# Seven half products instead of eight in the gate/up pairs of two feed-forward stages

## The reference

```python
h = h + 0.5 * swiglu(rmsnorm(h, g1), w_gate, w_up, w_down)   # stage 0 (layer 0), stage 2 (layer 1)
h = h + mixer(rmsnorm(h, gm));  h = h + cross_attn(rmsnorm(h, gx), mem_n, ...)
h = h + 0.5 * swiglu(rmsnorm(h, g2), ...)                    # stage 1 (layer 0), stage 3 (layer 1)
swiglu(x, w_gate, w_up, w_down) = (silu(x @ w_gate) * (x @ w_up)) @ w_down     # 1024 -> 2816 -> 1024
```

## Time and profile before

| | |
|---|---|
| median of three runs | 2180.11 us |
| profiled execution, span from first to last instruction | 2178.7 us |
| granted clock of TensorE, mean | 0.999 |
| PE busy, matmuls | 2169.0 us, 10582 |
| DVE / ACT / POOL busy | 1042.9 / 455.5 / 1529.9 us |
| weight stream moved | 202.03 MB of 214.12 |

### The profile page before, as it was taken

The page is one execution under the profiler, slowest core; times in us unless marked ns, Lnnn a source line. Parts: engine busy times, 40 slices in busy tenths (PEclk is TensorE's granted clock), DMA queues, the critical chain, the costliest instruction groups (busy, mean ns, idle before and its releaser), DMA issues. The chain is left out here.

```text
span 2178.7 us, 30347 instructions
## 1 busy us (share of the span) xinstructions
PE 2169.0 (100%) x10582; PEld 1793.5 (82%) x10582; DVE 1042.9 (48%) x1386; ACT 455.5 (21%) x816; POOL 1529.9 (70%) x1530
## 2 busy tenths in 40 slices
PE   9999999999999999999999999999999999999998
PEld 7888888888988888888888888886878888888887
DVE  6556795695444352233352224356872543222333
ACT  4001212034223210001131111134362332111112
POOL 7777787667964776776776677685756657667764
PEclk9999999999999999999999999999999999999999
DMA  5233323223431333333333333232322222333332
GB/s 196 95 96 116 115 97 122 91 77 98 129 92 59 102 97 96 96 96 97 111 102 96 96 96 97 96 102 78 102 88 92 78 68 96 97 97 97 97 97 82
DMA packets 115350, 214.12 MB, mean 98 GB/s; under 512 B 12832, under 2 KB 14400, under 8 KB 115008
## 3 DMA queue, kind: packets, MB, share of 16 engines
q1 hardware_dynamic: 111024, 202.03, 29.3%
q10 hardware_dynamic: 4240, 10.99, 1.5%
HBM read 208.77 MB, written 4.19 MB: 98 GB/s over the span
## 5 line engine op out<-in xcount | busy, mean ns | idle before, releaser
L443 PE MATMUL ps<-x,w_split 128*128 128x512 f32 (+1 forms) x2854 | 1105.4, 387 | 1.1 <-DVE x L1754 0.7
L445 PE MATMUL ps<-x,w_split 128*128 128x512 f32 (+1 forms) x2854 | 1097.2, 384 | 0.0
L444 PE MATMUL ps<-x,w_split 128*128 128x512 f32 (+1 forms) x2854 | 1096.9, 384 | 0.0
L401 POOL TENSOR_TENSOR w_split<-w_raw,w_split 128x512 fp32r<-128x512 f32 x758 | 1026.8, 1355 | 64.2 <-ACT w_split L1463 1.1
L391 POOL TENSOR_SCALAR w_split<-w_raw 128x512 fp32r<-128x512 f32 x754 | 495.1, 657 | 560.5 <-PE ps L445 556.4
L443 PEld LDWEIGHTS ps<-x,w_split 128*128 128x128 f32 x2854 | 536.0, 188 | 118.2 <-issue 10.3
L444 PEld LDWEIGHTS ps<-x,w_split 128*128 128x128 f32 x2854 | 536.2, 188 | 107.0 <-issue 1.4
L445 PEld LDWEIGHTS ps<-x,w_split 128*128 128x128 f32 x2854 | 536.1, 188 | 107.0
L1881 DVE TENSOR_TENSOR x<-arena,x 128x512 fp32r<-128x512 f32 x88 | 119.2, 1365 | 218.6 <-ACT x L1322 218.6
L1831 DVE TENSOR_TENSOR tu<-ps,rstd 128x512 f32<-128x512 f32 x88 | 60.7, 689 | 315.3 <-PE ps L445 315.3
L1260 ACT ACTIVATE sg<-tg 128x512 f32<-128x512 f32 x88 | 55.6, 632 | 668.5 <-DVE tg L1828 667.2
(11 more groups left out here) (303 smaller groups left out, 1332.5 us busy)
## 6 DMA issues: line engine op xcount, KB each, us to landing
w_raw<-in_stream SPq DMA_DIRECT2D x758, 256.0 KB, 2.6
arena<-in_memT ACTq DMA_DIRECT2D x2, 1024.0 KB, 6.4
s_tables<-kv ACTq DMA_DIRECT2D x4, 512.0 KB, 3.2
arena<-s_tables ACTq DMA_DIRECT2D x4, 512.0 KB, 4.3
out<-h ACTq DMA_DIRECT2D x6, 256.0 KB, 2.2
h<-in_xT SPq DMA_DIRECT2D x4, 256.0 KB, 5.3
h<-in_xT SPq DMA_DIRECT2D x2, 512.0 KB, 6.9
w_raw<-in_stream SPq DMA_DIRECT2D x5, 128.0 KB, 5.8
```

Source lines behind the costliest of these rows:

```text
L401: pool.tensor_tensor(lo, x, hi.bitcast(F32), ALU.subtract).then_inc(split_ready if half else S("half_split"), 1)
L443: pe.matmul(dst, wh, xh, start=start, stop=False)
L444: pe.matmul(dst, wh, xl, start=False, stop=False)
L445: return pe.matmul(dst, wl, xh, start=False, stop=stop)
```

## The change

Let A11, A21 be the first four channel chunks of the first and second 256 tokens, A12, A22 the last four chunks; B11 and B21 the first and last four chunks of the gate's weights, B12 and B22 those of the up's. From pair 3 on (`SEVEN = {1: 3, 3: 3}`: stages 1 and 3, pairs 3 to 21) a pair is formed by seven products of 4 chunks x 3 matmuls of 256 columns, in this order: A11 B11 (M1), S1 T1 (M5), S2 T2 (M6, added onto M1 in the same bank), S4 B22, S3 T3, A12 B21 (M2, a bank of its own), A22 T4, with the token sums S1 = A21 + A22, S2 = S1 - A11, S4 = A12 - S2, S3 = A11 - A21 and the weight sums T1 = B12 - B11, T2 = B22 - T1, T3 = B22 - B12, T4 = B21 - T2.

- **Weights.** `W` gets 6 more half units. ACT makes all seven high parts (before: POOL). DVE forms T1, T2 and T4 in PSUM banks 6, 7, 0 and their low parts; POOL forms T3 in a new SBUF tile and the low parts of B11, B22, T3 and B21. SP loads the halves in the order B11, B12, B22, B21, each when its raw half has been used.
- **Results.** ACT keeps three partial results in `sq` (c1, c5, c2), DVE adds them (`join`: C12, C22, C11), then `up_out`, `gate_out` and, after ACT's SiLU, the product.
- **Token sums.** During the norm ACT writes the gained `h` once more in float32 (8 copies); DVE forms the four sums and their low parts (1024 columns each), ACT their high parts. They lie in the chunks that the first hidden chunks used, so hidden chunks 0 to 3 are split only in the last pair.
- **Order.** The first down block takes its 8 outputs in another order (`DOWN_FIRST_SEVEN`). The tables of stage 1 go behind down chunks 10 and 16. Several semaphores of short steps are merged into `act_step` and `dve_step`, and DMA scratch is made smaller, with no other effect on the order.

The core of the diff, in the order PE, SP, POOL, ACT, DVE as in the file:

```diff
+            def seven(f, p):
+                g, u, n = FFN_AT[f] + 2 * p, FFN_AT[f] + 2 * p + 1, 3 * (seven_of(f, p) - 1)
+                again = p > SEVEN[f]
+                sp.wait_ge(S("half_split"), g - 1)
+                if again:
+                    sp.wait_ge(S("w_sum"), n + 1)
+                load(g, g % 2, 0)
+                sp.wait_ge(S("half_split"), u - 1)
+                load(u, u % 2, 0)
+                if again:
+                    sp.wait_ge(split_ready, g - 1)
+                    sp.wait_ge(S("w_sum"), n + 2)
+                else:
+                    sp.wait_ge(split_ready, u - 1)
+                load(u, u % 2, 1)
+                sp.wait_ge(split_ready, u - 1 if again else g - 1)
+                if again:
+                    sp.wait_ge(S("w_sum"), n + 3)
+                load(g, g % 2, 1)
...
+            def seven_prepare(f, p):
+                n = 7 * seven_of(f, p)
+                def low(name, high, sem):
+                    src = t3[:] if name == "T3" else raw_of(f, name)
+                    pool.wait_ge(S("u_hi"), n + high)
+                    pool.tensor_tensor(unit(f, name, 1), src, unit(f, name, 0).bitcast(F32), ALU.subtract
+                                       ).then_inc(sem, 1)
+                low("B11", 1, S("half_split"))
+                for name in ("B12", "B22"):
+                    pool.wait_ge(*raw_sem(f, p, name))
+                pool.tensor_tensor(t3[:], raw_of(f, "B22"), raw_of(f, "B12"), ALU.subtract).then_inc(S("w_sum3"), 1)
+                low("B22", 4, split_ready)
+                low("T3", 5, S("half_split"))
+                low("B21", 6, split_ready)
...
+                product(c21, "B11", tokens(1, 1), start=True).then_inc(S("m_done"), 1)
+                pe.wait_ge(S("u_lo"), 3 * q + 1)
+                pe.wait_ge(S("up_ready"), FC * f + p - 1)
+                if first:
+                    pe.wait_ge(S("s_lo"), n + 1)
+                product(c12, "T1", summed("S1"), start=True).then_inc(S("m_done"), 1)
+                pe.wait_ge(S("u_lo"), 3 * q + 2)
+                pe.wait_ge(S("m_kept"), 3 * q + 1)
+                if first:
+                    pe.wait_ge(S("s_lo"), n + 2)
+                product(c21, "T2", summed("S2")).then_inc(S("m_done"), 1)
+                pe.wait_ge(split_ready, at + 1)
+                pe.wait_ge(S("m_kept"), 3 * q + 2)
+                if first:
+                    pe.wait_ge(S("s_lo"), n + 3)
+                product(c12, "B22", summed("S4"), stop=True).then_inc(S("half_done"), 1)
+                pe.wait_ge(S("half_split"), at + 2)
+                pe.wait_ge(S("m_kept"), 3 * q + 3)
+                if first:
+                    pe.wait_ge(S("s_lo"), n + 4)
+                product(c21, "T3", summed("S3")).then_inc(S("block_done"), 1)
+                pe.wait_ge(split_ready, at + 2)
+                if not first:
+                    pe.wait_ge(S("m_joined"), 3 * q)
+                product(second, "B21", tokens(1, 2), start=True, stop=True).then_inc(S("half_done"), 1)
+                pe.wait_ge(S("u_lo"), 3 * q + 3)
+                pe.wait_ge(S("m_joined"), 3 * q + 2)
+                product(c21, "T4", tokens(2, 2), stop=True).then_inc(S("block_done"), 1)
...
+                if n in FFN_NORM and FFN_NORM.index(n) in SEVEN:
+                    sums_high(FFN_NORM.index(n), ("S1", "S2"))
...
+                    if name in ("B11", "T1", "T2"):
+                        if p > at:
+                            act.wait_ge(S("m_done"), 3 * (q - 1) + ("B11", "T1", "T2").index(name) + 1)
+                    else:
+                        act.wait_ge(S("half_done") if name in ("B22", "B21") else S("block_done"),
+                                    b - 1 if name in ("B22", "T3") else b)
+                    act.activation(unit(f, name, 0), src, ACT.Copy).then_inc(S("u_hi"), 1)
...
+                sums_high(f, ("S4", "S3"))
+                for p in range(at - 1):
+                    silu(p // 2, p % 2)
+                for name in ("B11", "T1", "T2", "B22"):
+                    high(at, name)
+                silu((at - 1) // 2, (at - 1) % 2)
+                for name in ("T3", "B21"):
+                    high(at, name)
+                for p in range(at, FC):
+                    high(p, "T4")
+                    if p > at:
+                        silu((p - 1) // 2, (p - 1) % 2)
+                    more = p + 1 < FC
+                    keep(p, "c1")
+                    if more:
+                        high(p + 1, "B11")
+                    keep(p, "c5")
+                    if more:
+                        high(p + 1, "T1")
+                    keep(p, "c2")
+                    if more:
+                        for name in ("T2", "B22", "T3", "B21"):
+                            high(p + 1, name)
...
+                    sums(FFN_NORM.index(n))
+                    sums_low(FFN_NORM.index(n), ("S1", "S2"))
...
+                def join(p, name):
+                    q, b = seven_of(f, p), FFN_AT[f] + 2 * p
+                    c11, c21, c12, c22 = gate_up(p)
+                    if name == "C12":
+                        dve.wait_ge(S("half_done"), b + 1)
+                        dve.wait_ge(S("m_kept"), 3 * q + 3)
+                        ins = dve.tensor_tensor(c12, c12, kept(p, "c2"), ALU.add)
+                    elif name == "C22":
+                        dve.wait_ge(S("block_done"), b + 1)
+                        ins = dve.tensor_tensor(c22, c21, kept(p, "c5"), ALU.add)
+                    else:
+                        dve.wait_ge(S("block_done"), b + 2)
+                        ins = dve.tensor_tensor(c11, second, kept(p, "c1"), ALU.add)
+                    ins.then_inc(S("m_joined"), 1)
+                def up_out(p):
+                    s = p % 2
+                    dve.wait_ge(S("m_joined"), 3 * seven_of(f, p) + 2)
+                    dve.wait_ge(S("hid_done"), FC * f + p - 1)
+                    dve.tensor_tensor(tu[:, s, :], ps[:, BANKS[2 * s + 1], :], rstd[:], ALU.mult
+                                      ).then_inc(S("up_ready"), 1)
+                def gate_out(p):
+                    s = p % 2
+                    dve.wait_ge(S("m_joined"), 3 * seven_of(f, p) + 3)
+                    dve.tensor_tensor(tg[:, s, :], ps[:, BANKS[2 * s], :], rstd[:], ALU.mult
+                                      ).then_inc(S("gate_ready"), 1)
+                def product(p):
+                    s = p % 2
+                    dve.wait_ge(S("up_ready"), FC * f + p + 1)
+                    dve.wait_ge(S("silu"), FC * f + p + 1)
+                    dve.tensor_tensor(hid[:, p, :], sg[:, s, :], tu[:, s, :], ALU.mult).then_inc(S("hid_done"), 1)
+                for p in range(at - 1):
+                    gate(p // 2, p % 2)
+                add(at, "T1")
+                add(at, "T2")
+                sums_low(f, ("S4", "S3"))
+                add(at, "T4")
+                low(at, "T1")
+                low(at, "T2")
+                gate((at - 1) // 2, (at - 1) % 2)
+                for p in range(at, FC):
+                    more = p + 1 < FC
+                    if p > at:
+                        join(p - 1, "C11")
+                        gate_out(p - 1)
+                    low(p, "T4")
+                    if more:
+                        add(p + 1, "T1")
+                    if p > at:
+                        product(p - 1)
+                    if more:
+                        add(p + 1, "T2")
+                        low(p + 1, "T1")
+                        add(p + 1, "T4")
+                        low(p + 1, "T2")
+                    join(p, "C12")
+                    join(p, "C22")
+                    up_out(p)
+                    if not more:
+                        dve.wait_ge(S("hid_done"), FC * f + 4)
+                        low_part(0)
+                        low_part(1)
+                join(FC - 1, "C11")
+                gate_out(FC - 1)
+                product(FC - 1)
+                low_part(2)
+                low_part(3)
```

More of the change, by code:

```diff
@@ L160 @@
 OUT_NORM = [2, 3, 6, 7]
+SEVEN = {1: 3, 3: 3}
+TABLES_BEHIND = (10, 16)
+SEVEN_BEFORE = {f: sum(FC - at for g, at in SEVEN.items() if g < f) for f in range(5)}
+SUM_BANKS = {"T1": 6, "T2": 7, "T4": 0}
+SECOND_BANK = 1
+HALF_T = T // 2
 XQ_BASE, OD_BASE = [13, 36], 21
@@ L232, with seven_units, seven_of, seven_at @@
 A_XPT = A_XP + 4 * T
+A_SUMS, A_GAINED = 6 * T, 14 * T
+def seven_units(f):
+    own, other = FFN_AT[f] % 2, 1 - FFN_AT[f] % 2
+    return {"B11": (8, 9), "T1": (10, 11), "T2": (12, 13), "B22": (4 * own, 4 * own + 2),
+            "T3": (4 * own + 1, 4 * own + 3), "B21": (4 * other, 4 * other + 2), "T4": (4 * other + 1, 4 * other + 3)}
+SEVEN_HELD = {"S1": 4, "S2": 6, "S4": 0, "S3": 2}
+def seven_of(f, p):
+    return SEVEN_BEFORE[f] + p - SEVEN[f]
+def seven_at(f):
+    return sorted(SEVEN).index(f)
+def is_seven(b):
+    return any(FFN_AT[f] + 2 * at <= b < FFN_AT[f] + 2 * FC for f, at in SEVEN.items())
```

(55 more changed lines are left out.)

244 lines of the change are left out of this document (185 added, 59 removed).

## The result

The changed kernel takes 2166.82 us in the median of four runs (2165.80 to 2170.73); the kernel before, run beside it, 2180.12. The ratio is 0.9942, with a 95% interval of 0.9928 to 0.9956. So the change gains 13.3 us, where 25.6 were forecast. The median lies 0.2 us inside the upper end of 2149 to 2167, in the part that belonged to rival A; the mean of the four, 2167.5, lies 0.5 us outside it. The profiled execution is the longest of the four: 2170.73 us, span 2168.9.

The account below looks back on a forecast made before the run. TensorE, busy 2169.0 of 2178.7 us, was taken as the bound: number of matmuls times their step. A gain of 30.5 us less 4.8 for edges is 25.7, so 2154.5 us was forecast, range 2149 to 2167.

Parts of the forecast that it names:

- rival A: One product in each pair waits 0.2 to 0.5 us, at product 3 or 7; 2160 to 2172 us; chance 0.22.
- Part 1: TensorE's matmuls: a pair falls from 10.88 to 10.07 us, 0.80 us gained in each of 38 pairs, 30.5 us.
- Rival C: Each product's first matmul pays 0.10 us, 0.70 us a pair; about 2181 us, no change; chance 0.04.
- Part 2: What the other engines must have ready in time within one new pair; no stall per pair was taken.
- I take no stall per pair: In seven-product pairs, TensorE never waits; the smallest margins were 0.3 to 0.5 us for c1, 0.7 for C22.
- rival B: T1 and product of every pair each meet a POOL subtraction, 1.82 us each; pair 10.8 to 11.15 us; chance 0.08.
- landing range: In each pair, the load of B12 lands 2.6 us after SP issues it, between 2.3 and 3.0.
- Part 3: Losses at the edges of stages 1 and 3: 2 x (0.9 + 1.2 + 0.3) = 4.8 us.
- the term for the first pair: First seven-product pair of each stage: B12 of pair 4 loads late, products 5 and 7 wait; 1.2 us (0 to 2).
- Start edge: Norm before each stage: two long DVE operations delay POOL's split of tile 3, TensorE waits 0.9 us (0 to 3).
- End edge: End of each stage: low parts of hid 0 and 1 meet POOL's split of the first down block; 0.3 us (0 to 1.5).
- Tables: Stage 1's angle tables on DVE, moved behind down tiles 10 and 16, cost nothing; with less lead 8.4 us each.

Follow-up runs that it names:

- x1: The changed kernel with SP loading B12 once T3's sum has read it, instead of after T3's low part: 2159.61 us, ratio 0.9904.
- x2: The changed kernel with POOL's low part of B11 waiting for DVE's product of the pair before: 2162.30 us, ratio 0.9916.
- x5: The changed kernel with DVE's product, pairs 4 to 20, waiting until POOL has made the next pair's low part of B11: 2195.44 us, ratio 1.0068.
- x4: The changed kernel with pair 2's gate out (DVE) and SiLU (ACT) earlier, low parts of S4 and S3 later, around pair 3: 2158.25 us, ratio 0.9900.
- x7: x6 with DVE's low parts of S1 and S2 moved from the norm to behind the first two pairs' gates: 2155.05 us, ratio 0.9884.
- x3: The changed kernel with TensorE's pairs 4 to 21 as a hardware loop over two pairs instead of written out: 2163.88 us, ratio 0.9925.
- x8: x7 with x3's hardware loop for TensorE's pairs 4 to 21: 2155.46 us, ratio 0.9883.
- x9: x7 with the sums' low parts spread over the first two pairs and c2 kept before T1's copy in pair 3: 2158.05 us, ratio 0.9896.
- x6: The changed kernel with the edits of x1 and x4 together: 2155.22 us, ratio 0.9882.

## Why the forecast was off by half

**The matmuls (Part 1)** were right to 0.01 us: 10.08 us a pair against 10.07, at full granted clock in every pair. Rival C (0.10 us per product) is refuted by the 84 even steps.

**The order within a pair (Part 2)** was right: counted from the start of the pair at 819.86, T1 at 2.2 to 2.9 (2.1 to 2.8 forecast), product 2.8 to 3.5 (2.7 to 3.4), both at 0.70 and 0.68 us. Rival A's small wait in every pair does not exist; the time fell into its range for other reasons. (That range was added up some 2 us low: 0.3 to 0.6 a pair give 2162 to 2173.) That the median lies inside 2149 to 2167 is luck, since two terms were too small by 7.2 and 8.5 us in the profiled execution, 2168.9 us of span against 2153.0 forecast.

**"I take no stall per pair" failed.** I gave the product 0.2 us to spare before low B11; it was 0.19 at most, and in four pairs it was gone. But that is not the step that failed: I priced one lost port as "C22 ends at 8.4 to 8.5, still just in time", and in the four pairs in which the product alone loses it, C22 ends at 8.1, in time. What I left out is a load so late that T1 itself starts behind low B11 (2.89 us into the pair). Then T1 loses the port, and the product behind it as well: rival B's two prices in one pair, C22 at 9.8, 1.34 us. I had the earlier trace rows' landing range of 2.3 to 3.0 us and took it as a limit; it was taken with at most one instruction fetch in each of these stages, and the change itself brings 13 or 14. The term I left out is 7.2 us in the profiled execution (no pair of x1 shows it, and those of x2 0.18 us each). Rival B's price per pair was good: with the product late in every pair, x5 takes 11.0 us a pair, where B had 10.8 to 11.15. Its sum, at most 2195 against 2195.4, is partly chance: x5 loses 5.7 us against the kernel before in its pairs 4 to 20 and 9.3 in the two first pairs, for which B's sum had no such term.

**The edges (Part 3): the term for the first pair failed**, 1.2 us each forecast, 5.6 and 5.3 measured, 8.5 us over both stages. I followed ACT there and only one thing on it, T3's copy behind the SiLU. That showed where I said, at products 5 and 7 (2.0 and 1.8 us together, where I had 1.2). I did not write out DVE's queue ahead of pair 3, where the low parts of S4 and S3 (4.12 us for two, both against POOL) stand between T2 and gate out. That brings the wait at product 2 and, through SiLU and three copies, the 2.2 us at product 3. x4, which changes only this order, shortens the two first pairs by 7.7 us together.

**Start edge**: 0.9 forecast, 0.65 measured, and x7 shows its cause, DVE's low parts against POOL's split. **End edge**: 0.3 forecast, 0 found. **Tables**: nothing, as forecast.

So of the 12.3 us that are missing in the median, 8.5 are the first pairs, and the start and end edges give 1.1 back. That leaves 4.9 for long pairs and slow last matmuls, where the profiled execution, the longest, has 7.2 and 1.6; the others were not traced, so how this splits in them is inferred. x1's median fits: it is 7.2 less, 5.3 without its shorter pair 3.

## What to carry to other kernels

Write out every engine's queue for the first round of a new steady state as well as for the steady state itself: what is left of the old order stands in front of it, and here it cost 10.9 us in two rounds. Where two engines share a port, ask of each operation what falls behind it when it loses: here the last one in a row had the slack (1.8 us instead of 0.7 cost nothing), the one before it had not, since it makes both lose. The price of a late load was 0.18 us without the port and 1.34 with it, so fix the order by an earlier load or a wait. Code that is written out brings its own DMA traffic, which has to be counted among the transfers it runs beside. And where one execution differs from the next by 1 us or so at the kernel's ends, an account by stage says more than the difference of two medians.

## What the runs showed of the hardware that was not expected

The granted clock of TensorE fell to the level of 1.2 GHz for some 3.4 us in pair 3 of stage 3 of x1, right behind the two waits of products 2 and 3 (1.47 and 2.29 us from one matmul to the next). The 3.4 us are an estimate from the second row, 4.40 us at 0.61. The matmuls of 256 columns then started 0.21 us apart instead of 0.12, which is why pair 3 stayed at 15.24 us. Columns as above, with the clock behind POOL's:

```profile
1829.00:1835.60 6.60, 3.40 (x27) 2.99 (x25) 5.67 (x8) 2.55 (x6) 1.86 (x3) 1.00 0.15 56
1835.60:1840.00 4.40, 4.40 (x24) 4.40 (x25) 3.47 (x5) 2.14 (x5) 4.19 (x4) 0.61 0.29 81
1840.00:1845.00 5.00, 5.00 (x44) 5.00 (x43) 2.82 (x7) 2.31 (x4) 3.74 (x3) 1.00 0.46 142
```

In x2, x3 and x5 the first pairs of both stages show it too, behind two waits like these (1.0 to 1.3 and 2.3 us), and in x8 that of stage 3, behind a single wait of 2.03 us. The changed kernel has nearly the same two waits (1.32 and 2.29 us) and shows 1.00 all through its pair 3; x7 has the single wait of 2.03 us and x9 one of 2.41, and both show 1.00. So what decides is left open; but a stall on TensorE can cost more than its own length: x8's pair lasts 13.54 us, where x7's, with the same wait, lasts 12.49. In x4 and x6, where the longest step is 1.4 us, the clock is 1.00 throughout the first pairs. The slow last matmuls of three traces show the same level at another place.
